# Three weight tiles instead of two, the low part written over the loaded one, and the split placed six blocks later

## What is computed

```python
def mixer_block(h, ...):
    xn = rms_norm(h, norm1_g)
    proj = xn @ w_in
    fq, fk, fv, ff, cq, ckv, krope, sq, sk, sv, gates = jnp.split(proj, offsets, axis=-1)
    ...
    log_decay = jnp.cumsum(jax.nn.log_sigmoid(ff + fox_forget_b), axis=1)
    out_a = causal_block_attention(fq, fk, fv, log_decay)          # 8 heads of 64, with decay
    ...
    out_b = causal_block_attention(q, k, v_mla)                    # 8 heads, low-rank q and kv, rope
    ...
    out_c = sliding_window_attention(sq, sk, sv, swa_sinks, ...)   # 8 heads, window 128
    g = jax.nn.sigmoid(gates.reshape(B, L, N_BRANCH, D_MODEL))
    y = jnp.einsum('blnc,ncd->blnd', branches, w_branch)
    return h + jnp.sum(g * y, axis=2) @ w_o

def conv_ffn(h, norm2_g, w_up, conv_w, conv_b, w_down):
    u = rms_norm(h, norm2_g) @ w_up
    c = conv_b + sum(conv_w[i] * pad(u)[:, i:i + L] for i in range(3))
    gate, val = jnp.split(c, 2, axis=-1)
    return h + (jax.nn.silu(gate) * val) @ w_down
```

## Time and profile before

| | before |
| --- | --- |
| median of 3 runs | 1980.91 us |
| lowest and highest run | 1980.17, 1981.82 us |
| span of the profiled execution | 1979.4 us |
| TensorE busy | 97% |
| VectorE, ScalarE, GpSimd busy | 59%, 39%, 52% |

### The profile page before, as it was taken

The page is one execution under the profiler, slowest core; times in us unless marked ns, Lnnn a source line. Parts: engine busy times, 40 slices in busy tenths (PEclk is TensorE's granted clock), DMA queues, the critical chain, the costliest instruction groups (busy, mean ns, idle before and its releaser), DMA issues.

```text
span 1979.4 us, 36478 instructions
## 1 busy us (share of the span) xinstructions
PE 1914.7 (97%) x14396; PEld 1817.1 (92%) x14396; DVE 1159.0 (59%) x2121; ACT 766.2 (39%) x1514; POOL 1025.5 (52%) x1306
## 2 busy tenths in 40 slices
PE   7899999999999999999998999999999999999999
PEld 7889998888999999999997899988889999999887
DVE  7665476787465666552256654767874655665411
ACT  5455666655223222220044556666553232222100
POOL 7655454544364444544477455544443645445553
PEclk9999999999999999999999999999999999999999
DMA  4212121211232322332332121112112423323332
GB/s 149 75 44 65 54 65 44 63 45 55 65 129 85 97 86 86 97 93 93 93 109 76 43 65 54 63 46 65 45 53 65 141 86 97 97 86 96 96 97 96
DMA packets 44802, 156.30 MB, mean 79 GB/s; under 512 B 5012, under 2 KB 5268, under 8 KB 44504
## 3 DMA queue, kind: packets, MB, share of 16 engines
q1 hardware_dynamic: 44488, 153.75, 24.7%
q10 hardware_dynamic: 144, 0.22, 0.0%
HBM read 149.63 MB, written 4.26 MB: 78 GB/s over the span
## 4 chain that ended last, share of the span: by engine, by line
PE 77%; DVE 12%; ACT 4%; issue 3%; POOL 2%; DMA 1%; SPq 0%; DVEq 0%; ACTq 0%; POOLq 0%
PE ps L1357 20%; PE ps L1360 19%; PE ps L1362 19%; PE ps L1588 5%; PE ps L1372 2%; PE ps L1368 2%; PE ps L1371 2%; PE ps L1376 2%; DVE osum L1993 1%; DVE rstd L1691 1%; PE ps L1540 1%; PE ps L1501 1%; POOL wl L817 1%; DVE ps L1962 1%; DVE square L1686 1%
## 5 line engine op out<-in xcount | busy, mean ns | idle before, releaser
L817 POOL TENSOR_TENSOR wl<-raw,wh 128x256 fp32r<-128x256 f32 x1076 | 798.7, 773 | 746.5 <-DVE wh L1670 739.9
L1357 PE MATMUL ps<-xh,wh 128*128 128x264 f32 (+1 forms) x2880 | 810.7, 303 | 12.5 <-DVE wl L1750 9.4
L1360 PE MATMUL ps<-xl,wh 128*128 128x264 f32 (+1 forms) x2880 | 764.3, 286 | 0.0
L1362 PE MATMUL ps<-xh,wl 128*128 128x264 f32 (+1 forms) x2880 | 585.4, 285 | 0.0
L1357 PEld LDWEIGHTS ps<-xh,wh 128*128 128x128 f32 x2880 | 546.7, 190 | 31.1 <-issue 18.3
L1360 PEld LDWEIGHTS ps<-xl,wh 128*128 128x128 f32 x2880 | 547.4, 190 | 17.0 <-issue 8.9
L1362 PEld LDWEIGHTS ps<-xh,wl 128*128 128x128 f32 x2880 | 451.2, 190 | 0.0
L1670 DVE CAST wh<-raw 128x1024 fp32r<-128x1024 f32 x270 | 206.6, 765 | 176.0 <-PE ps L1357 89.1
L1588 PE MATMUL ps<-pt,vx 128*128 128x512 f32 (+7 forms) x480 | 157.8, 409 | 3.9 <-ACT pt L1274 2.3
L1985 DVE TENSOR_TENSOR ps<-ps,cst 128x128 f32<-128x128 f32 (+6 forms) x240 | 74.8, 313 | 145.3 <-PE ps L1546 111.0
L1274 ACT ACTIVATE pt<-ps 128x256 f32<-128x256 f32 (+5 forms) x224 | 78.5, 363 | 112.5 <-DVE ps L1985 111.2
(11 more groups left out here) (194 smaller groups left out, 3440.9 us busy)
## 6 DMA issues: line engine op xcount, KB each, us to landing
raw<-weights SPq DMA_DIRECT2D x270, 512.0 KB, 3.5
h<-tokens SPq DMA_DIRECT2D x4, 528.0 KB, 6.9
h<-tokens SPq DMA_DIRECT2D x8, 264.0 KB, 6.0
residual<-h SPq DMA_DIRECT2D x8, 264.0 KB, 5.0
h<-residual SPq DMA_DIRECT2D x8, 264.0 KB, 5.9
out<-h SPq DMA_DIRECT2D x8, 256.0 KB, 4.7
cst<-constants SPq DMA_DIRECT2D x1, 1048.0 KB
extra<-positions SPq DMA_DIRECT2D x18, 4.1 KB
```

The source lines that it names most:

```text
L817: ins = nc.gpsimd.tensor_tensor(wl[c % SPLIT][:, part], raw[:, c % RAW, part], wh[c % SPLIT][:, part].bitcast(F32), ALU.subtract)
L1357: a = nc.tensor.matmul(out, a_hi, x_hi[:, sl], start=first, stop=False)
L1360: nc.tensor.matmul(out, a_hi, x_lo[:, sl], start=False, stop=False)
L1362: ins = nc.tensor.matmul(out, a_lo, x_hi[:, sl], start=False, stop=last)
```

## The change

- `raw` becomes a ring of three tiles, and `wl` is placed at the same addresses: the low part of a chunk overwrites the chunk as loaded, piece by piece. Together with wh there are six chunk tiles instead of eight, 8 KB per partition less.
- A load may thus start only when PE is done with the chunk whose low part lies there. SP's load of chunk c+2 now waits until PE has started chunk c (`s_start`), and is issued at the first block of chunk c. In the prologue chunks 0, 1 and 2 are loaded instead of 0 to 3.
- The high part and the low part of chunk c+2 are placed at the seventh block of chunk c (SPLIT_AT = 6) on VectorE and GpSimd, not at the first. The prologue's high part of chunk 2 is left out, since it comes at block 6.
- Each of GpSimd's four pieces increments `s_lo`; PE waits at every second block, for the piece with this block: 1080 waits instead of 270.
- The third entry of START is 17 instead of 4.

```diff
-RAW, SPLIT = 2, 3
+RAW, SPLIT = 3, 3
+PIECE = 2
+PIECES = BLK // PIECE
+SPLIT_AT = 6
...
-START = [12, 16, 4, 18, 21, 26, 11]
+START = [12, 16, 17, 18, 21, 26, 11]
...
+    raw_at = at[0]
     raw = sb("raw", [P, RAW, CW])
+    wl = [sb(f"wl{i}", [P, CW], F32R, offset=raw_at + i * CW * 4) for i in range(RAW)]
     wh = [sb(f"wh{i}", [P, CW], F32R) for i in range(SPLIT)]
-    wl = [sb(f"wl{i}", [P, CW], F32R) for i in range(SPLIT)]
...
                 if n >= RAW:
-                    sp.wait_ge(s_lo, n - RAW + 1)
+                    sp.wait_ge(s_start, n - RAW + 2)
...
-                if n % BLK == 0:
-                    load(n // BLK + AHEAD + RAW)
+                if n % BLK == 0 and n > 0:
+                    load(n // BLK + AHEAD)
...
-            for n in range(2, AHEAD + RAW):
+            for n in range(2, RAW):
                 load(n)
...
-                for a in range(0, CW, CW // 4):
-                    part = slice(a, a + CW // 4)
-                    ins = nc.gpsimd.tensor_tensor(wl[c % SPLIT][:, part], raw[:, c % RAW, part],
-                                                  wh[c % SPLIT][:, part].bitcast(F32), ALU.subtract)
-                ins.then_inc(s_lo, 1)
-                began["last"] = (s_lo, c + 1)
+                for a in range(0, CW, CW // PIECES):
+                    part = slice(a, a + CW // PIECES)
+                    nc.gpsimd.tensor_tensor(wl[c % RAW][:, part], raw[:, c % RAW, part],
+                                            wh[c % SPLIT][:, part].bitcast(F32), ALU.subtract).then_inc(s_lo, 1)
+                began["last"] = (s_lo, PIECES * (c + 1))
...
-                if n % BLK == 0:
+                if n % BLK == SPLIT_AT:
                     chunk_low(n // BLK + AHEAD)
...
-                if n % BLK == 0:
-                    pe.wait_ge(s_lo, c + 1)
+                if n % PIECE == 0:
+                    pe.wait_ge(s_lo, n // PIECE + 1)
...
-                if n % BLK == 0 and n > 0:
+                if n % BLK == SPLIT_AT:
                     high_part(n // BLK + AHEAD)
...
                     nc.vector.tensor_tensor(wl[0][:, :], raw[:, 0, :], wh[0][:, :].bitcast(F32), ALU.subtract).then_inc(
-                        s_lo, 1)
+                        s_lo, PIECES)
                 elif k == 3:
                     high_part(1)
-                elif k == 6:
-                    high_part(2)
```

More of the change, by code:

```diff
@@ L1346, in weights @@
                 c = n // BLK
-                if n % BLK == 0:
-                    pe.wait_ge(s_lo, c + 1)
+                if n % PIECE == 0:
+                    pe.wait_ge(s_lo, n // PIECE + 1)
                 a = n % BLK * P
-                return wh[c % SPLIT][:, a:a + P], wl[c % SPLIT][:, a:a + P]
+                return wh[c % SPLIT][:, a:a + P], wl[c % RAW][:, a:a + P]
             def gemm(n, slot, x_hi, x_lo, first, last, skip=0):
```

## The result

| | before | after |
| --- | --- | --- |
| median | 1981.37 us (4 runs) | 1989.07 us (4 runs) |
| lowest and highest | 1980.17, 1982.13 us | 1988.56, 1989.64 us |
| profiled span | 1979.4 us | 1987.1 us |

A forecast was written before the change was run, and what follows sets the result against it. TensorE was taken to be busy 1914.7 of 1979.4 us, leaving 64.7 idle. Terms 0 + 7.0 + 2.5 + 3.4 - 3.0 = +9.9 us gave a span of 1989.3, stated as 1990.5 us; range 1981 to 1998.

The forecast's parts named there:

- full stages, 810 waits: Full stages such as w_o and FFN up: additional TensorE waits nearly always met, taken as 0 (0 to 4 us).
- waits at chunks 52 and 187: TensorE stalls about 3.5 us at each, the low part now behind GpSimd's heads' low copy: +7.0 us (6.2 to 7.8).
- slow clock behind them: Stretches at granted clock 0.50 after the stalls at chunks 52 and 187: +3.4 us (0 to 7).
- starts of the layers: Chunks 6 and 141 late by 3.5 and 3.1 us, part coming back: +2.5 us kept (0 to 5).
- mixer, casts moved: Six high casts, together 6.1 us, leave the mixer's chain of waits; half taken: -3.0 us (-6 to 0).
- narrowest, 39 and 174: Chunks with least slack where copies and low parts swap places: 0 to 0.5 us each, taken as 0.
- waits of over 2 us: TensorE waits in the earlier trace: five have a half-clock stretch beside them, one has none; basis of the clock charge.
- GpSimd's part: Layer starts: low part behind the extra-row copies, chunk 6 at 61.4 (+3.5 us), chunk 141 +3.1 us.
- up to 1 us: Layer start: the cast taken from the prologue lets the first steps come this much earlier.
- the prediction's own sign: TensorE's idle time in 60 to 480 falls by 0 to 3 us a layer; 6 or more means Rival B.
- Rival B: Mixer: the ring of two holds it, freeing it gives -13 + 7.0 = -6, 1975 us; chance 0.12.
- Rival A: Stalls at chunks 52 and 187 without slow clock, layer starts absorbed, casts give 6.1: +0.9, 1982 us; chance 0.20.

The follow-up runs named there:

- order52: Changed kernel with GpSimd's low parts of chunks 52 and 187 placed four blocks earlier, ahead of the heads' low copy: 1979.38 us, ratio 0.9986.
- low6: load6 with low parts of chunks 6 and 141 ahead of the extra-row copies; those of 52 and 187 landed behind the heads' copy: 1983.40 us, ratio 1.0005.
- late_only: Kernel before with only the high and low parts of chunk c+2 placed at the seventh block of chunk c, old rings kept: 2015.64 us, ratio 1.0173.
- whole: Changed kernel with TensorE waiting once per chunk for the whole low part, 270 waits: 2008.19 us, ratio 1.0131.
- filled52: Changed kernel with 28 additional matmuls, results unused, on TensorE ahead of its wait at chunks 52 and 187: 1988.61 us, ratio 1.0039.
- low6_filled: low6 with 28 additional matmuls, results unused, ahead of TensorE's wait at chunks 52 and 187: 1980.77 us, ratio 0.9999.
- load6: order52 with the third entry of START 18 instead of 17, so the load of chunks 6 and 141 precedes the decay rows: 1982.29 us, ratio 1.0002.
- pieces_only: Kernel before with only the count per piece and TensorE waiting at every second block, 1080 waits instead of 270: 1982.15 us, ratio 1.0002.
- high2: Kernel before with chunk 2's high part taken out of the prologue and put, with its low part, at block 6: 1983.89 us, ratio 1.0011.
- ring4: Changed kernel with four shared tiles, high and low parts back at the first block, loads one chunk further ahead, third START entry 10: 1979.79 us, ratio 0.9988.

## Why the prediction was right

The forecast was +9.9 us on the profiled execution and 1990.5 us; it became +7.7 and 1989.07. By its steps, each read from the table of lateness or from a wait in it, so they add up only roughly:

| term | forecast | measured between chunks |
| --- | --- | --- |
| full stages, 810 waits | 0 | +0.3 (53 to 140), -0.5 (188 to 269) |
| waits at chunks 52 and 187 | +7.0 | 3.47 + 3.46 |
| slow clock behind them | +3.4 | 1.6 + 1.6 |
| starts of the layers | +2.5 | 0.0 (to 12), -1.7 (140 to 147) |
| mixer, casts moved | -3.0 | -2.7 (12 to 51), +1.8 (147 to 186) |

**The main term** was right in place, mechanism and size. It came out of two views: the order, which showed the copy ahead of the low part, and the timeline, which showed that the copy's own input is TensorE's last matmul of the chunk before. order52 confirms it by 10 us from one move in each layer. The chunks that the prediction called narrowest, 39 and 174, lost 0.4 and 0.6 us, where 0 to 0.5 each had been named and 0 taken.

**The clock** was charged by counting stretches behind waits. (Of the five "waits of over 2 us" with a stretch beside them in the kernel before, two are 1.97 and 1.96 us.) Both stretches appeared at 1.6 us each. That the idle time brings them is likely, not certain: of four such waits of 3.5 us left idle, in the changed kernel and in low6, three had a stretch behind them, as had all four waits of 5.5 us in late_only and whole; of four that were filled, in filled52 and low6_filled, none had. A gain in time from filling, 1.4 and 1.5 us against the kernel before of each chip, lies within the intervals. That low6 escaped one stretch means that the forecast of both had some luck. Nor does the term cover the clock of the whole kernel. Away from the two places the changed kernel's profile has 17.0 us at half clock and that of before 20.4, which is worth some 1.7 us and was not forecast.

**The starts of the layers** are the term that was mis-sized, +2.5 forecast and -1.7 measured. GpSimd's part was nearly as worked out: chunk 6 at 60.3 where 61.4 was said, chunk 141 3.3 us later in its layer where 3.1 was said. But the forecast wait of 3 us for the low part came only at chunk 6, with 2.12 us. At chunk 141 TensorE did not wait for it: it had lost the time ahead, at vt, and the first piece was done at 1054.0, 0.3 us before it began the chunk. That the number agrees there is luck. Two things were missed. The load behind the decay rows blocks VectorE ahead of vt, for which TensorE waits 2.81 us in layer 0 and 4.16 in layer 1; load6 shows that this hides behind the late low part and costs nothing of its own. And more came back: chunk 3 was 3.6 us early, where "up to 1 us" was written for the cast taken out of the prologue; 1.6 us of it is shorter waits and the rest mostly a slow stretch that did not occur. Of 5.2 us at chunk 142 four were gone at 147: a wait for ScalarE's ptm fell from 1.67 to 0.18 us, one for VectorE's nm from 2.06 to 1.63, and the half-clock stretch of 3.4 us at 1102.5 in the profile of before has no like in that of after. The same wait for nm in layer 0, 2.08 us at 111.22, fell to 1.62, again without the stretch. All nine kernels with the later placement have this wait at 1.62 or 1.63 us in both layers and no stretch behind it; the four others have it at 2.06 to 2.08, and three of these have the stretch. So about 2 us a layer come from the later placement, and the table books them under the starts.

**The casts** were forecast to gain 3.0 us and the mixers gained 0.9, of which little is theirs. (Each single cast moved six blocks later; the prediction's "two blocks earlier" is true only of the row of casts as a whole, where each takes the place two blocks ahead of its successor's old one.) The mechanism is there, at single places. The wait at 299.95 in layer 0 is shorter, before and after:

```profile
299.95 0.39 PE L1540 MATMUL ps<-xq,xk 97*128 97x256 f32 x1 [1.97 <-ACT ptm L1255]
```

```profile
299.16 0.39 PE L1543 MATMUL ps<-xq,xk 97*128 97x256 f32 x1 [0.94 <-ACT ptm L1258]
```

1.0 us went there, and as much at the same step of layer 1 (2.04 to 1.01). Every kernel with the later placement has this wait at 0.94 or 0.95 us in layer 0, and every one with the old placement at 1.97 to 2.00. But 1.6 us are lost again between chunks 37 and 51, where the same kernels wait longer for ScalarE and VectorE (0.86 to 1.46 us at chunk 47, 0.62 to 1.03 at 41, and 0.49 and 0.34 that were not there). And the profile of before has a half-clock stretch of 6.8 us behind 300.4, which costs 2.7 to 2.9 us against pieces_only, high2 and ring4, whose casts stand at the old place and which have none. That is the whole of the -2.7. In layer 1 the changed kernel has a stretch of 3.4 us at 1292.5 that before's has not. Without the clock the moved casts gain nothing over these chunks, and that the term looks partly right is luck. By the prediction's own sign, TensorE's idle time in 60 to 480 fell by 1.5 us and in 1060 to 1480 by 1.8, within the 0 to 3 a layer that it named.

Rival B, that relieving the ring would free the mixer by 13 us, needed 6 us or more of that sign; and ring4, where the loads wait for TensorE too and the casts stay in their old place, gains 4.4 us at most. Rival A, no clock loss and a full return of the casts, is refuted by the two stretches.

**What was luck.** The sum missed by 2.2 us because two misses went opposite ways: the starts came out 4.2 us lower than forecast and the casts 2.1 us higher. The main term, and so the direction, does not rest on this.

What I had not foreseen is the balance within the change. The prediction let TensorE wait for one piece only at chunks 52 and 6 and a layer on, and so used the pieces, but it nowhere says what they are worth. They are worth nothing alone (pieces_only) and 18 to 19 us behind the later split (whole).

## What to carry to other kernels

When a step of a pipeline moves to a later place in an engine's list, look for what it has been moved behind, and at what that waits for: if it waits for the very engine that the step feeds, the move costs the whole chain behind that engine's last instruction, once for each such place, however much slack the averages show. A cure is to move only those few steps back; here four of 270 low parts and two loads turned a loss of 0.4% into a gain of 0.45%. And release in small pieces is insurance: it does nothing while the producer is early, and limits the wait to the first piece when it is late.

## What the runs showed of the hardware

Where a wait of 3.5 us on TensorE was filled with useless matmuls, the granted clock of the next 3.5 us was 1.00 where it was 0.51 (low6 and low6_filled at chunk 52), the 2.4 GHz level instead of the 1.2 GHz level. But the same wait of 3.47 us in low6 at chunk 187 had a clock of 1.00 behind it without any filling. So the length of a wait does not settle whether a slow stretch follows, and less so for shorter waits: in the changed kernel a stretch of 3.4 us began 1.6 us after a wait of 1.01 us at 1290.93, and the wait of 2.0 to 2.1 us at L1540 in layer 1 had none behind it in the profile of before, 3.4 us in ring4's and 6.8 us in those of pieces_only and high2, so single profiles of like kernels differ by 1.7 to 3.4 us for this alone. And 810 additional met waits on TensorE, three for each chunk, could not be seen in the time (ratio 1.0002, 0.9993 to 1.0011).
